# Attention in a two-layer decoder trunk: the reciprocal sums of the softmax are spread over the rows by a store to DRAM and a broadcast load, not by TensorE products and a ScalarE copy

## What is computed

```python
# latent attention, for each block of 128 queries i: keys 0 .. 128*(i+1)
sc = q @ k.T * scale                 # causal
pr = softmax(sc)                     # exp(sc - max) / sum
y_mla = pr @ v
# sliding window, for each block of 128 queries i: keys of blocks i-1 and i, and a sink
pr = softmax(concat([sc, sink]))[..., :-1]
y_swa = pr @ v
y = concat([y_ssd, y_mla, y_swa]) @ w_out
x = x + g1 * y
```

## Time and profile before

| | us |
|---|---|
| median of 3 runs | 2313.07 (2312.45 to 2313.55) |
| the profiled execution | 2314.43 |
| its span, first to last instruction | 2312.7 |
| TensorE busy in the span | 2258.6 |
| VectorE busy | 1631.5 |
| ScalarE busy | 1103.8 |
| GpSimd busy | 1023.0 |

### The profile page before, as it was taken

How to read it: one execution, slowest core, us unless ns; L and a number is a source line. 1 busy time by engine, 2 the same in 40 slices (tenths; PEclk the granted TensorE clock), 3 DMA queues, 4 the chain that set the end, 5 groups by cost and what they waited for, 6 DMA issues and landing times.

```text
span 2312.7 us, 31034 instructions
## 1 busy us (share of the span) xinstructions
PE 2258.6 (98%) x11401; PEld 1849.8 (80%) x11401; DVE 1631.5 (71%) x2098; ACT 1103.8 (48%) x1817; POOL 1023.0 (44%) x660
## 2 busy tenths in 40 slices
PE   6999999999999999999999999999999999999998
PEld 5888867887788888888878787788878888888887
DVE  7985468449866676778898744772796767667886
ACT  5355557434444444444543464772454444444455
POOL 3222369345887777300002124053389777760000
PEclk7999999999999999999999999999999999999999
DMA  9742243342333333487557232114323333347763
GB/s 329 283 131 70 63 119 120 110 137 64 103 118 96 118 95 112 151 286 255 149 209 248 64 74 65 41 55 155 111 75 94 114 91 114 94 134 262 257 205 114
DMA packets 271301, 317.13 MB, mean 137 GB/s; under 512 B 33613, under 2 KB 188032, under 8 KB 270383
## 3 DMA queue, kind: packets, MB, share of 16 engines
q1 hardware_dynamic: 269359, 312.11, 41.6%
q10 hardware_dynamic: 1072, 2.23, 0.5%
q0 software_dynamic: 720, 0.81, 0.1%
HBM read 248.37 MB, written 62.54 MB: 134 GB/s over the span
## 4 chain that ended last, share of the span: by engine, by line
PE 86%; DVE 7%; issue 2%; ACT 1%; DMA 1%; SPq 1%; POOL 1%; DVEq 0%; POOLq 0%; ACTq 0%
PE bank L1580 31%; PE bank L1126 19%; PE bank L1595 17%; PE bank L1186 6%; PE bank L1422 1%; PE bank L1345 1%; PE bank L1471 1%; DVE hLo L2245 1%; SPq L538 1%; DVE xT L2239 1%; DMA adaw<-in_ada_w_dram 1%; PE bank L1276 1%; DVE xT L2580 1%; DVE tLo L2649 1%; PE bank L1254 1%
## 5 line engine op out<-in xcount | busy, mean ns | idle before, releaser
L1046 POOL TENSOR_TENSOR wLo<-raw,wHi 128x1024 fp32r<-128x1024 f32 x66 | 161.2, 2444 | 405.4 <-ACT wHi L1048 405.4
L1773 POOL TENSOR_TENSOR prodLo<-comb,prodHi 128x512 fp32r<-128x512 f32 x160 | 234.2, 1471 | 120.8 <-ACT prodHi L1088 120.8
L1580 PE MATMUL bank<-tHi,prodHi 128*128 128x512 f32 x640 | 251.0, 392 | 4.2 <-DVE tLo L2649 4.2
L1580 PE MATMUL bank<-tLo,prodHi 128*128 128x512 f32 x640 | 250.1, 391 | 0.0
L1580 PE MATMUL bank<-tHi,prodLo 128*128 128x512 f32 x640 | 250.0, 391 | 0.0
L1595 PE MATMUL bank<-gateHi,downHi 128*128 128x512 f32 x616 | 240.3, 390 | 0.0
L1595 PE MATMUL bank<-gateHi,downLo 128*128 128x512 f32 x616 | 239.7, 389 | 0.0
L1595 PE MATMUL bank<-gateLo,downHi 128*128 128x512 f32 x616 | 239.7, 389 | 0.0
L1088 ACT ACTIVATE prodHi<-comb 128x512 fp32r<-128x512 f32 x160 | 100.5, 632 | 248.9 <-PE bank L1580 229.9
L2594 DVE SCALAR_TENSOR_TENSOR ub<-bank,ffp,ub 128x1023 f32<-128x1023 f32 x88 | 112.8, 1282 | 141.8 <-ACT ub L2052 140.2
L1580 PE MATMUL bank<-hHi,prodHi 128*128 128x512 f32 x480 | 187.1, 390 | 5.9 <-POOL prodLo L1773 3.3
(11 more groups left out here) (424 smaller groups left out, 5428.9 us busy)
## 6 DMA issues: line engine op xcount, KB each, us to landing
raw<-in_ffn_w_up_dram SPq DMA_DIRECT2D x88, 512.0 KB, 4.8
gateRaw<-gateOut SPq DMA_DIRECT2D x154, 256.0 KB, 4.2
adaE<-in_ada_w_dram SPq DMA_DIRECT2D x64, 512.0 KB, 6.4
gateOut<-gateSums SPq DMA_DIRECT2D x22, 1024.0 KB, 5.5
raw<-in_w_in_dram SPq DMA_DIRECT2D x34, 512.0 KB, 4.1
downRaw<-in_ffn_w_down_dram SPq DMA_DIRECT2D x66, 256.0 KB, 3.6
raw<-in_w_out_dram SPq DMA_DIRECT2D x28, 512.0 KB, 3.9
downCols<-in_ffn_w_down_dram SPq DMA_DIRECT2D x24, 512.0 KB, 3.6
```

The source lines that it names most:

```text
L1046: eng.tensor_tensor(lo[:], raw[slot][:], fview(hi[:]), ALU.subtract).then_inc(s["split_lo"], 1)
L1580: last = mm(o, w[idx][:, c0], moving(idx, kp, hi), start=kp == 0 and q_ == 0, stop=kp == 3 and q_ == 2)
L1773: pool.tensor_tensor(sLoW[idx][:], product_source(js, idx), fview(sHiW[idx][:]), ALU.subtract).then_inc(s["us_lo"], 1)
```

## The change

- The four products of `inverse_sums` and the ScalarE copy go, 16 times in each layer. In their place SyncE makes `spread_inverse(n)` for each pair: it waits for the reciprocal, stores the 128 x 4 values to DRAM turned round (each piece 4 bytes), waits until they have landed, and issues two loads of 64 rows x 2 x 128 values, each with all rows the same, into one of four `invSum` buffers.
- `att_scaled` moves from u - 1 to u - 2 in VectorE's loop, `att_lo` from u - 3 to u - 4, `att_hi` on ScalarE from u - 2 to u - 3.
- In the first layer SyncE makes `spread_inverse` of n = 0 to 9 between the loads of `ada_w`, as `ADA_AMONG` says: n = 0 after tile 3, then after tiles 4, 5, 7, 8, 10, 11, 12, 14 and 15. In the second layer it makes n = 0 to 9 first, and only then `store_rstd`, `spread_rstd` and the first two packs. In both, n = 10 to 15 stand ahead of pack 22 and the loads of x.
- The output projection makes the parts 4 and 5 of both its first packs last.

```diff
+INV_AHEAD = 10
+ADA_AMONG = (4, 5, 6, 8, 9, 11, 12, 13, 15, 16)
...
+            def spread_inverse(n):
+
+                kind, i = DONE[n]
+                sp.wait_ge(s["sw_r" if kind == "s" else "ml_r"], nth("sw_r" if kind == "s" else "ml_r", i + 1))
+                sp.dma_start(inv_out[n].rearrange("h t -> t h"), stat[kind][:, i % 3, 2, :], allow_slow_non_contiguous=True).then_inc(s["inv_stored"], 16)
+                if n >= 4:
+                    kind4, i4 = DONE[n - 4]
+                    sp.wait_ge(s["sw_x" if kind4 == "s" else "ml_x"], nth("sw_x" if kind4 == "s" else "ml_x", i4 + 1))
+                sp.wait_ge(s["inv_stored"], nth("inv_stored", 16 * (n + 1)))
+                for q in range(2):
+                    sp.dma_start(bcs[n % 4][64 * q:64 * q + 64, :].rearrange("p (r t) -> p r t", r=2),
+                                 inv_out[n].rearrange("(r q) t -> q r t", q=2)[q:q + 1].to_broadcast([64, 2, BLK])).then_inc(s["inv_loaded"], 16)
...
                 if n == N_OUT0 and onward:
-                    load_ada(range(2, ADA_PACKS))
+                    for n_, r in enumerate(ADA_AMONG):
+                        load_ada(range(ADA_AMONG[n_ - 1] if n_ else 2, r))
+                        spread_inverse(n_)
+                    load_ada(range(ADA_AMONG[-1], ADA_PACKS))
                     sp.wait_ge(s["ada_used"], nth("ada_used", ADA_PACKS))
-                if n == N_OUT0 + 2 and not onward:
+                if n == N_OUT0 and not onward:
+                    for n_ in range(INV_AHEAD):
+                        spread_inverse(n_)
+                if n == N_OUT0 and not onward:
                     store_rstd()
                     spread_rstd()
+                if n == N_OUT0 + 2:
+                    for n_ in range(INV_AHEAD, 2 * NB):
+                        spread_inverse(n_)
...
-            def inverse_sums(kind, i):
-
-                pe.wait_ge(s["sw_r" if kind == "s" else "ml_r"], nth("sw_r" if kind == "s" else "ml_r", i + 1))
-                for h in range(4):
-                    last = mm(att_bank(kind)[64 * (h % 2):64 * (h % 2) + 64, 256 + (h // 2) * P:256 + (h // 2 + 1) * P],
-                              stat[kind][:, i % 3, 2, h:h + 1].to_broadcast([P, 64]), ident[:], start=True, stop=True)
-                last.then_inc(s["sw_b" if kind == "s" else "ml_b"], 1)
...
-                    kind, i, _ = UNITS[u - 1]
-                    if LAST[kind][i] == u - 1:
-                        inverse_sums(kind, i)
...
-            out_steps(0, (3, 6, 7, 4, 5))
-            out_steps(1, (0, 1, 2, 3, 6, 7, 4, 5))
+            out_steps(0, (3, 6, 7))
+            out_steps(1, (0, 1, 2, 3, 6, 7))
+            out_steps(0, (4, 5))
+            out_steps(1, (4, 5))
...
-                A(bcs[n % 2][:], half(3, 0 if kind == "s" else 1)[:, 256:512], ACT.Copy).then_inc(s["sw_c" if kind == "s" else "ml_c"], 1)
...
-                    for w, todo in ((u - 1, copy_inverse), (u - 2, att_hi)):
-                        if 0 <= w < NU and LAST[UNITS[w][0]][UNITS[w][1]] == w:
-                            todo(UNITS[w][0], UNITS[w][1])
+                    w = u - 3
+                    if 0 <= w < NU and LAST[UNITS[w][0]][UNITS[w][1]] == w:
+                        att_hi(UNITS[w][0], UNITS[w][1])
...
+                if i >= 3:
+                    dve.wait_ge(s["inv_stored"], nth("inv_stored", 16 * (N_INV[kind][i - 3] + 1)))
                 dve.reciprocal(st_[:, 2, :], st_[:, 1, :]).then_inc(s["sw_r" if kind == "s" else "ml_r"], 1)
...
-                dve.wait_ge(s["sw_c" if kind == "s" else "ml_c"], nth("sw_c" if kind == "s" else "ml_c", i + 1))
+                dve.wait_ge(s["inv_loaded"], nth("inv_loaded", 32 * (n + 1)))
...
-                for w, todo in ((u, inverse_of), (u - 1, att_scaled), (u - 3, att_lo)):
+                for w, todo in ((u, inverse_of), (u - 2, att_scaled), (u - 4, att_lo)):
```

More of the change, by code:

```diff
@@ L316, in build @@
     stat = {k: place(f"stat_{k}", [P, 3, 3, 4], F32, R[13] + 8320 + 192 * n) for n, k in enumerate("sm")}
-    bcs = [place(f"invSum{i}", [P, 256], F32, R[11] + K * i) for i in range(2)]
+    bcs = [place(f"invSum{i}", [P, 256], F32, a) for i, a in enumerate((R[11], R[11] + K, R[15] + K, R[15] + 2 * K))]
     ytk = [place(f"attOut{i}", [P, 256], F32, R[11] + 2 * K + K * i) for i in range(2)]
@@ L397, in build @@
     rstd_out = nc.dram_tensor("rstdOut", [1, 2 * NB, P], F32, kind="Internal").ap()
+    inv_out = nc.dram_tensor("invOut", [2 * NB, 4, BLK], F32, kind="Internal").ap()
     gate_out = nc.dram_tensor("gateOut", [P, 7, NK, HALF], F32, kind="Internal").ap()
@@ L513, in build @@
         sw_vt sw_vcopied sw_m k_rope un_s un_n un_e un_half un_ta un_t un_ca un_cd un_o
-        sw_r sw_b sw_c sw_x sw_hi sw_lo ml_r ml_b ml_c ml_x ml_hi ml_lo
+        sw_r sw_x sw_hi sw_lo ml_r ml_x ml_hi ml_lo inv_stored inv_loaded
         cum_stored cum_loaded sd_xe sd_t sd_c sd_xt sd_xd sd_bt sd_cb sd_seg sd_dec sd_M sd_yd sd_yd_read sd_eb sd_o sd_st sd_y
@@ L750, in norm_sums, with att_bank @@
             return half(1 if i == 3 else 3, 1)[:, 0:NB]
+        def att_bank(kind, i):
+            return half(3, 0 if kind == "s" else 1)[:, 0:256]
         def out_pair(t):
@@ L1437, in transposes @@
                 turn(1).then_inc(s["un_t"], 1)
-            def att_bank(kind):
-                return half(3, 0 if kind == "s" else 1)
             def values(u):
@@ L1459, in values @@
                             for h in (2 * pair, 2 * pair + 1):
-                                last = mm(att_bank("s")[64 * (h % 2):64 * (h % 2) + 64, pair * P:(pair + 1) * P], svt[:, i - 1 + b, 64 * pair:64 * pair + 64],
+                                last = mm(att_bank("s", i)[64 * (h % 2):64 * (h % 2) + 64, pair * P:(pair + 1) * P], svt[:, i - 1 + b, 64 * pair:64 * pair + 64],
                                           pt[u % 4][:, (2 * h + b) * P:(2 * h + b + 1) * P], start=b == (0 if i else 1), stop=b == 1)
@@ L1470, in values @@
                             src = pt[u % 4][:, q * HALF + b * P:q * HALF + (b + 1) * P] if len(hs) == 2 else pt[(first_u, u)[q] % 4][:, b * P:(b + 1) * P]
-                            last = mm(att_bank("m")[64 * q:64 * q + 64, pair * P:(pair + 1) * P], vt[:, b, h * 64:(h + 1) * 64], src, start=b == 0, stop=b == i)
+                            last = mm(att_bank("m", i)[64 * q:64 * q + 64, pair * P:(pair + 1) * P], vt[:, b, h * 64:(h + 1) * 64], src, start=b == 0, stop=b == i)
                 last.then_inc(s["un_o"], 1)
-            def inverse_sums(kind, i):
-                pe.wait_ge(s["sw_r" if kind == "s" else "ml_r"], nth("sw_r" if kind == "s" else "ml_r", i + 1))
-                for h in range(4):
-                    last = mm(att_bank(kind)[64 * (h % 2):64 * (h % 2) + 64, 256 + (h // 2) * P:256 + (h // 2 + 1) * P],
-                              stat[kind][:, i % 3, 2, h:h + 1].to_broadcast([P, 64]), ident[:], start=True, stop=True)
-                last.then_inc(s["sw_b" if kind == "s" else "ml_b"], 1)
             y_hi = [yHi[:, j, :] for j in range(4)] + [mHi[:, j, :] for j in range(2)] + [sHi[:, j, :] for j in range(2)]
@@ L1981, in exps @@
                     A(prs[i % 2][:, :, 256], nsink[:], ACT.Copy).then_inc(s["sw_m"], 1)
-            def copy_inverse(kind, i):
-                act.wait_ge(s["sw_b" if kind == "s" else "ml_b"], nth("sw_b" if kind == "s" else "ml_b", i + 1))
-                n = N_INV[kind][i]
-                if n >= 2:
-                    act.wait_ge(s["sw_x"], nth("sw_x", N_INV_S[n - 1]))
-                    act.wait_ge(s["ml_x"], nth("ml_x", n - 1 - N_INV_S[n - 1]))
-                A(bcs[n % 2][:], half(3, 0 if kind == "s" else 1)[:, 256:512], ACT.Copy).then_inc(s["sw_c" if kind == "s" else "ml_c"], 1)
             def att_hi(kind, i):
@@ L1996, in _ @@
             exps(0)
-            for u in range(NU + 2):
+            for u in range(NU + 3):
                 def finish():
@@ L2501, in att_scaled @@
                     dve.wait_ge(s["ml_lo"], nth("ml_lo", n - 1 - N_INV_S[n - 1]))
-                dve.tensor_tensor(ytk[n % 2][:], half(3, 0 if kind == "s" else 1)[:, 0:256], bcs[n % 2][:], ALU.mult).then_inc(s["sw_x" if kind == "s" else "ml_x"], 1)
+                dve.tensor_tensor(ytk[n % 2][:], att_bank(kind, i), bcs[n % 4][:], ALU.mult).then_inc(s["sw_x" if kind == "s" else "ml_x"], 1)
             def att_lo(kind, i):
@@ L2524, in _ @@
             least(1)
-            for u in range(NU + 3):
+            for u in range(NU + 4):
                 if u in (SUMS_AT[1], TURN_AT) + NEXT_AT:
```

4 lines of the change are left out of this document (2 added, 2 removed).

## The result

The changed kernel takes **2538.4 us** (median of 4 runs, 2536.4 to 2543.9), the kernel before beside it 2313.3 (2312.5 to 2316.4): a ratio of **1.097** (95% interval 1.0954 to 1.0994), 225 us more. I had said 2314.3, with 2330 as the upper end.

What follows compares the result with a forecast made beforehand. TensorE was taken as the bound, with VectorE nearly as tight in the first layer. First layer +2.3 and second -1.1 sum to +1.2 us: 2315.6 against the profiled execution, 2314.3 against the median; 80% range 2301 to 2330.

Steps and rivals of the forecast that it cites:

- The store, 2.4 us: Round trip of the reciprocals: 512 pieces of 4 bytes land in DRAM 2.4 us after issue, range 1.4 to 4.5.
- My own sign of failure: The prediction fails if the store lands in over 4 us, or if VectorE nowhere waits for invSum.
- the slower rival: Writing 512 4-byte pieces takes 2 us more than taken, round trip over 7 us, total 2328 us; chance 0.26.
- 13 ns a piece: Cost of each small DMA piece, from 3533 packets in 4 us; 0.4 us for 512 pieces on 16 engines.
- Loads: After the store: second load issued 0.5 us after the first, landing 2.1 us later; whole round trip 5.2 us.
- SyncE's turn: SyncE held 3.3 us by each store-and-loads pair; in the first layer, tiles late and GpSimd about 5 us behind.
- 4 us remain: At the end, pack 22 and x go out some 10 us later, wanted some 8 us later; about 4 us slack.
- TensorE's saving, 18.2 us: Removed products in both layers give at most 30 x 0.54 + 2 x 1.00 us, 9.1 us a layer.
- First block: First layer, block 1 waits for m0's scaling: TensorE loses 2.5 us; idle VectorE ahead of it 0.6 us.
- m4 behind the rstd loads: First layer: m4's store queues behind spread_rstd and tile 15, landing 4.5 us later; VectorE waits 5.4 us.
- Second layer about nothing: Rstd row moved past ten spreads: +0.4 us up to unit 26, where ScalarE idles 3 to 4; layer -1.1 us.
- First layer: Stalls to m4 come to +6.0 us, the last six pairs give back 3.7: +2.3 us for the layer.

Runs made afterwards that it cites:

- e1: Kernel before with six probe DMAs of different forms, one after the other, in SyncE's idle time of the second layer; 2314.6 us, one run.
- e3: Changed kernel storing 2 KB of constants in 16 pieces of 128 bytes instead of the reciprocals, all else as in the change; 2329.6 us, ratio 1.0082.
- e11: Changed kernel with its turned store kept, but VectorE's product takes a constant tile and waits for no load; 2453.1 us, ratio 1.0602.
- e10: Changed kernel with the 2 KB constant store in 16 pieces, and VectorE's product on a constant tile, waiting for no load; 2324.8 us, ratio 1.0052.
- e6: Changed kernel with in-line store, one 2 KB broadcast load to 128 partitions, two half products on VectorE, two buffers for four; complete computation; 2353.2 us, ratio 1.018.
- e5: Kernel before with seven probe stores at different distances between pieces, in SyncE's idle time of the second layer; 2316.6 us, one run.

## Why the prediction was wrong, by its own steps

- **The store, 2.4 us, with 1.4 and 4.5 as ends: this is the step that failed.** It measured 9.2 us alone and up to 14.4 behind other transfers. My own sign of failure, a store that lands in over 4 us, came true. The mechanism that the slower rival names, 4-byte writes that take longer than I take, was the right one, with 2 us where it was 6.8. The lower part of the estimate (13 ns a piece, 0.4 us for 512) came from *loads*, in pieces of 130 bytes in the mean; e1 shows that it holds for reads (2.1 us) and nearly for spaced writes (2.4 and 2.5), and not for packed ones. The upper end was 3.1 plus 1.4 from rows of other kinds: a sum of two numbers, with nothing in it that bounds a packed write. I had written that no row shows a store in such pieces, and then let the range end where rows end.
- **Loads.** I took 0.5 for the second issue and 2.1 to landing; both issues take 1.24 to 1.31 us and the landing 2.6 at least (3.8 in the median and 10.2 at most in the kernel after; 2.6 and 3.8 in e3). The first round trip came to 14.3 us from the store's issue to `att_scaled` (332.67 to 346.95) where I had 5.2. With e3's cheap store the same distance was 4.8 (332.51 to 337.31). Behind the store that leaves 5.1 us in the kernel after and 3.5 in e3 where I had 2.8: a smaller miss, beside the 6.8 us of the store.
- **SyncE's turn.** I had it held for 3.3 us by each pair; it was 9.0 to 15.6, 11.2 in the median. In kind the places that I named are right: tiles late for GpSimd, the rstd row moved past ten spreads, x and pack 22 behind six. At 3.3 us they were a few us; at 11 they are enough for 64 and 70 us even where nobody waits for the loads (e11). Of the "4 us remain" at the end (pack 22, x) nothing was left there: 28.3 us of waiting in e11.
- **TensorE's saving, 18.2 us.** The work at full clock falls by 6.8 + 6.1 = 12.9 us. The distance of 0.54 us from one record to the next is not what went with the group: 12.9 / 32 is 0.40. Why it is less, no run shows; ends of matmuls are modelled.
- **What held** was the small-number part, which e3 tests with its cheap store. First block: 0.51 us of VectorE's wait where I had 0.6. m4 behind the rstd loads: 6.7 where I had 5.4. Second layer about nothing: +0.9, where I had -1.1. But not its reason, and so this agreement is luck. GpSimd's normalisation starts at 1536.54 in e3, 67 us after the first scores, where I had 66; but ScalarE's wait for it at u = 26 is 0.2 us and not 3 to 4, with 1.4 us at u = 21, where I had none. It gets there no sooner, and the gain is eaten, as e10 shows, by idle time of TensorE behind the other engines. First layer +12.5, where I had +2.3: my sum has one term for each stall and none for what follows it, such as the lower clock (8.6 us in e3, 3.4 before).
- **The clock** was in the prediction as a width only. It is a term: after a stall of some us, work goes on at 1.2 GHz. It took 60.0 us in the kernel after (6.8 before).
- **Sums.** Two of the prediction's are off by a rounding: the rstd row's chain adds up to 1522.8 and not 1522.9, and the chance above 2317.7 to 0.35 and not 0.34. Nothing hangs on either. And VectorE's wait in the first block comes to 1.1 us by its own figures (338.2 less 337.6 - 0.5), where the prediction names 0.6.

ScalarE's two waits for the scan's input in e3, at u = 21 and u = 26:

```profile
1540.98 1.06 ACT L2013 ACTIVATE ssdHi<-xbc 128x1024 fp32r<-128x1024 f32 x1 [1.43 <-POOL xbc L1738]
...
1558.72 1.06 ACT L2013 ACTIVATE ssdHi<-xbc 128x1024 fp32r<-128x1024 f32 x1 [0.24 <-POOL xbc L1738]
```

## What to carry to other kernels

Don't store single 4-byte elements packed in DRAM on a path that something waits for: here it took 9 us for 2 KB, 3 with one value's gap between them, 1.4 as 16-byte pieces. Store in line and let the reading engine's access pattern do the turn, as e6 does, though here even that lost to the kernel before. Where the trace has no row for a new operation, a sum of unlike rows is no upper end: ask what is new in kind (a write, packed, from many partitions), and leave the range open on that side by as much as a wait of that kind would cost at its worst place. A round trip by DMA has two prices, the latency for the one who waits and the time on the issuing queue for all that stands behind it, and here the second was enough by itself for 64 to 70 us a layer; to either, TensorE's clock after the stall is to be added.

## What the runs showed of the hardware

- Stores of 4-byte pieces, SBUF to DRAM, in a quiet moment: 9.2 to 9.9 us for 512 packed, 6.6 and 7.5 for 128 packed, 8.1 packed side by side; 3.0 every 8 bytes (3.6 side by side), 3.3 every 16, 1.8 every 32, 2.5 and 2.4 every 64 and 512. In the packed case nothing of the DMA engines shows as busy for most of that time (share 0.00 in the windows from 1472.0 to 1477.6 of e5).
- A store of 2 KB in good form lands in 1.3 to 1.6 us, and in 5.8 behind 1.5 MB of others on the same queue.
- A stretch of lower clock doesn't end with the stall: in the first layer of the kernel after, 4 us of full work followed at 1.2 GHz.
